# Feed-forward products of a hybrid decoder trunk, formed from seven block products instead of eight

## The reference

```
def _swiglu(x, w_gu, w_down):
    a, b = jnp.split(x @ w_gu, 2, axis=-1)          # w_gu 1024 x 5632
    return (jax.nn.silu(a) * b) @ w_down            # w_down 2816 x 1024

for i in range(DEPTH):                              # 2
    x = x + 0.5 * _swiglu(_rmsnorm(x, norm_g[i, 0]), ffn_gu[i, 0], ffn_down[i, 0])
    x = x + mixer(_rmsnorm(x, norm_g[i, 1]))        # retention, then gated delta
    x = x + 0.5 * _swiglu(_rmsnorm(x, norm_g[i, 2]), ffn_gu[i, 1], ffn_down[i, 1])
return _rmsnorm(x, final_g), new states
```

## Time and profile before

| | |
|---|---|
| median of 3 runs | 2621.64 us (2612.52 to 2621.98) |
| span of the profiled execution | 2619.2 us |
| TensorE busy, matmuls | 2572.6 us, 98% |
| VectorE busy | 1264.2 us, 48% |
| ScalarE busy | 821.0 us, 31% |
| GpSimd busy | 300.5 us, 11% |
| HBM traffic | 93 GB/s over the span |

### The profile page before, as it was taken

One profiled execution on the slowest core, in us unless ns is written; L12 is line 12 of the kernel. 1 busy time (PEld: TensorE's weight loads), 2 busy tenths in 40 slices (PEclk: granted clock), 3 DMA queues, 4 the chain that ended last, 5 costly groups with the idle time before them and its releaser, 6 DMA issues.

```text
span 2619.2 us, 48630 instructions
## 1 busy us (share of the span) xinstructions
PE 2572.6 (98%) x20575; PEld 2484.8 (95%) x20575; DVE 1264.2 (48%) x1584; ACT 821.0 (31%) x1042; POOL 300.5 (11%) x307
## 2 busy tenths in 40 slices
PE   8999999999999999999999999999999998999998
PEld 8999999898989899999999999989998998999998
DVE  5444334646464654443244443377557755444422
ACT  4222222424242432222232222244433344222222
POOL 1000010202020210000000000002530353000000
PEclk9999999999999999999999999999999999999999
DMA  4332334524242333332343323321122111323232
GB/s 131 96 96 76 88 93 141 185 86 177 93 173 97 137 91 87 96 86 78 97 111 91 96 82 89 104 84 52 49 66 87 36 49 53 97 84 93 78 91 74
DMA packets 340333, 246.73 MB, mean 94 GB/s; under 512 B 9428, under 2 KB 320908, under 8 KB 340208
## 3 DMA queue, kind: packets, MB, share of 16 engines
q1 hardware_dynamic: 325856, 197.32, 25.6%
q0 software_dynamic: 14352, 47.58, 5.0%
HBM read 218.81 MB, written 26.05 MB: 93 GB/s over the span
## 4 chain that ended last, share of the span: by engine, by line
PE 95%; DVE 3%; ACT 1%; issue 0%; DMA 0%; SPq 0%; ACTq 0%; DVEq 0%
PE ps L743 61%; PE ps L934 17%; PE ps L1118 5%; PE ps L828 1%; PE ps L851 1%; PE ps L837 1%; PE ps L1062 1%; PE ps L1128 1%; PE ps L783 1%; PE ps L1099 1%; DVE wl L1672 1%; PE ps L1075 1%; PE ps L993 0%; DVE xl L1678 0%; DVE cv L2012 0%
## 5 line engine op out<-in xcount | busy, mean ns | idle before, releaser
L743 PE MATMUL ps<-xh,wh 128*128 128x260 f32 x2816 | 569.0, 283 | 3.7 <-DVE gate L2258 1.5
L743 PE MATMUL ps<-xh,wl 128*128 128x260 f32 x2816 | 568.3, 284 | 0.0
L743 PE MATMUL ps<-xl,wh 128*128 128x260 f32 x2816 | 567.5, 283 | 0.0
L1672 DVE TENSOR_TENSOR wl<-raw,wh 128x2048 fp32r<-128x2048 f32 (+1 forms) x204 | 428.7, 2102 | 266.7 <-ACT wh L1333 266.5
L1333 ACT ACTIVATE wh<-raw 128x2048 fp32r<-128x2048 f32 (+1 forms) x204 | 354.5, 1738 | 343.2 <-PE ps L743 189.2
L743 PEld LDWEIGHTS ps<-xh,wh 128*128 128x128 f32 x2816 | 435.4, 189 | 5.8 <-issue 2.7
L743 PEld LDWEIGHTS ps<-xh,wl 128*128 128x128 f32 x2816 | 435.1, 189 | 0.0
L743 PEld LDWEIGHTS ps<-xl,wh 128*128 128x128 f32 x2816 | 433.8, 189 | 0.0
L743 PE MATMUL ps<-hh,wh 128*128 128x260 f32 x1408 | 284.4, 283 | 0.0
L743 PE MATMUL ps<-hh,wl 128*128 128x260 f32 x1408 | 283.1, 282 | 0.0
L743 PE MATMUL ps<-hl,wh 128*128 128x260 f32 x1408 | 282.8, 282 | 0.0
(11 more groups left out here) (372 smaller groups left out, 2857.8 us busy)
## 6 DMA issues: line engine op xcount, KB each, us to landing
raw<-in_ffn_gu_dram SPq DMA_DIRECT2D x176, 512.0 KB, 4.9
raw<-in_ffn_down_dram SPq DMA_DIRECT2D x64, 384.0 KB, 3.5
raw<-in_ret_w_in_dram SPq DMA_DIRECT2D x48, 512.0 KB, 4.4
raw<-in_ffn_down_dram SPq DMA_DIRECT2D x64, 320.0 KB, 3.9
s_ring<-in_state_ret_dram POOLq DMA_DIRECT2D x32, 512.0 KB, 6.2
out_dram<-s_ring POOLq DMA_DIRECT2D x32, 512.0 KB, 3.4
raw<-in_gdn_w_in_dram SPq DMA_DIRECT2D x32, 512.0 KB, 4.5
raw<-in_ret_w_out_dram SPq DMA_DIRECT2D x16, 512.0 KB, 3.8
```

Source lines behind the costliest of these rows:

```text
L743: m_ = nc.tensor.matmul(ps[:, 2 * q + h, 0:HALF], w_, v[:, kt0 + t, h * HALF:(h + 1) * HALF], start=b_, stop=e_)
L1672: nc.vector.tensor_tensor(wl[:, s, 0:cols], raw[:, s, 0:cols], wh[:, s, 0:cols].bitcast(F32), ALU.subtract).then_inc(w_low, 1)
```

## The change

All four feed-forwards are rewritten. In each, two K tiles, two output tiles and two token halves make a 2 x 2 by 2 x 2 block product, which is formed by Winograd's form of Strassen's scheme from seven products instead of eight. One feed-forward becomes 38 unrolled jobs (NJ): 22 gate jobs (gate and up tile of one index are the two output tiles; 4 pairs of K tiles) mixed with 16 down jobs (4 pairs of output tiles, in four rounds over the pairs of inner tiles that are ready: 2, 3, 3 and 3).

- TensorE: `products_of` gives the order of products in job j: 1, 2, 5, 6, then 4 of the job before, 3, 7. Each product is kp pairs x 3 passes of 128 x 128 x 260 into one bank; products 6, 3, 7 and 4 add onto what stands there.
- GpSimd: `block_sum` forms four sums of weight blocks per job, in order 1, 3 (for the job after the next), 2, 4 (for the next). It also forms sums T1 to T4 of the four blocks of h of a pair, `XG` for a down job, and the sums of squares.
- ScalarE and VectorE: `block_split` forms high and low parts of seven weight blocks per job in groups A (two blocks), 1, 2, 4, L (two); `h_split` those of the seven blocks of h of a pair, in three groups; `x_split` those of x ahead of a feed-forward.
- ScalarE copies the running sums out of a bank (m1, m5, u2); VectorE forms the outputs from banks and copies (C11, C12, C22, hA, hB; X11, X12, X21, X22 for down). The lower right output's last sum (C22) is formed by VectorE from the bank of product 7 and the copy m5.
- The mixers keep their code; their buffers move to other places.

```diff
+def ffn_jobs():
+    out = []
+    for q0, q1, pairs_ in ((0, 6, (0, 1)), (6, 12, (2, 3, 4)), (12, 18, (5, 6, 7)), (18, 22, (8, 9, 10))):
+        out += [("G", q, (0, 1, 2, 3)) for q in range(q0, q1)] + [("D", m, pairs_) for m in range(4)]
+    return out
+def products_of(j):
...
+    return [(j, 1), (j, 2), (j, 5), (j, 6), (j - 1, 4), (j, 3), (j, 7)]
...
+            def block_sum(f, j, n):                                    # GpSimd
+                r_, s_ = raw_blocks(f, j), mixed_block(j)
+                a11, a12, a21, a22 = r_[:, 0, :, 0, :], r_[:, 0, :, 1, :], r_[:, 1, :, 0, :], r_[:, 1, :, 1, :]
+                tt = nc.gpsimd.tensor_tensor
...
+                    m_ = tt(s_, a21, a22, ALU.add)
+                if n == "3":
+                    m_ = tt(a21, a11, a21, ALU.subtract)
+                if n == "2":
+                    pool.wait_ge(blk_low, blocks_split(f, j, "A"))
+                    pool.wait_ge(blk_sum, blocks_summed(f, j, "1"))
+                    m_ = tt(a11, s_, a11, ALU.subtract)
+                if n == "4":
+                    pool.wait_ge(blk_low, blocks_split(f, j, "1"))
+                    pool.wait_ge(blk_sum, blocks_summed(f, j, "2"))
+                    m_ = tt(s_, a12, a11, ALU.subtract)
...
+                for j in range(NJ + 1):                                # GpSimd, ffn
...
+                    if odd:
+                        v(f"hB.{b}")
...
+                        did(tt(parts[:, 6, :], parts[:, 5, :], parts[:, 2, :], ALU.subtract), f"T3.{e}")
+                        own(f"T1.{e}")
+                        did(tt(parts[:, 7, :], parts[:, 5, :], parts[:, 1, :], ALU.subtract), f"T2.{e}")
...
+                    if nxt:
+                        block_sum(*nxt, "2")
+                    if odd and j != LATE:
+                        fourth()
+                    if gated_b and not odd:
...
+                        did(tt(parts[:, 1, :], parts[:, 2, :], parts[:, 0, :], ALU.subtract), f"T1.{e}")
+                    if nxt:
+                        block_sum(*nxt, "4")
+                    if j > LATE:
+                        square_added(NORM_OUT[f], 2 * (j - LATE - 1))
+                    if j < NJ and not is_gate(j):
...
+                        did(tt(xt, xt, kept[:, 0:2, :], ALU.add), f"XG.{j}")
+                    if nxt2:
+                        block_sum(*nxt2, "1")
+                        block_sum(*nxt2, "3")
...
+                def product(c, m, steps=None):                         # TensorE
...
+                    o = ps[:, bank_of(c, m), 0:HALF]
+                    for t in steps:
...
+                        for n, (w_, r_) in enumerate(((hi_w, high), (hi_w, low), (lo_w, high))):
+                            m_ = nc.tensor.matmul(o, w_, r_, start=m in (1, 2, 5) and t == 0 and n == 0,
+                                                  stop=t == kp - 1 and n == 2, skip_group_check=m in (3, 4, 6, 7))
...
+            def block_split(f, j, group):                              # VectorE
+                dve.wait_ge(blk_high, blocks_split(f, j, group))
+                nc.vector.tensor_tensor(split_ends(wl, j, group), split_from(f, j, group), split_ends(wh, j, group).bitcast(F32),
+                                        ALU.subtract).then_inc(blk_low, 1)
...
+                for j in range(NJ + 1):                                # VectorE, ffn
...
+                    if j:
+                        t_(f"7.{b}")
+                        act_(f"m5.{b}")
+                        if gated_b:
+                            did(tt(kept[:, 2, :], bank(b, 7), kept[:, 3, :], ALU.add), f"C22.{b}")
...
+                    if gated_b:
+                        scaled_by_norm(b, "sr")
+                    if j:
...
+                        lower_second(b)
...
+                    if j < NJ:
+                        upper(j)
+                    low("A")
+                    low("1")
+                    if ending:
+                        tile_done(f, 2 * m)
+                    low("2")
+                    if odd:
+                        h_split(2, e)
+                    if j:
+                        lower(b)
+                    if j < NJ:
+                        upper_second(j)
...
+                    low("4")
...
+                    if is_gate(j):
+                        scaled_by_norm(j, "gr")
+                    if ending:
+                        tile_done(f, 2 * m + 1)
+                    if gated_b:
+                        h_split(3 if odd else 1, e)
+                    low("L")
...
```

More of the change, by code:

```diff
@@ new lines, in ffn_a_names @@
+def ffn_a_names():
+    out = []
+    for j in range(NJ):
+        b, gated = j - 1, is_gate(j - 1)
+        e, odd = (JOBS[b][1] // 2, JOBS[b][1] % 2) if gated else (0, 0)
+        out += ([f"silu.{b}"] if gated else []) + [f"m1.{j}", f"m5.{j}"]
+        if j == LATE:
+            out += [f"k2.{e}", f"k3.{e}", f"u2.{j}"]
+            continue
+        out.append(f"u2.{j}")
+        if odd:
+            out.append(f"k2.{e}")
+        if gated:
+            out.append(f"k3.{e}" if odd else f"k1.{e}")
+    return " ".join(out)
@@ new lines, in ffn_p_names @@
+def ffn_p_names():
+    out = []
+    for j in range(NJ + 1):
+        b, gated = j - 1, is_gate(j - 1)
+        e, odd = (JOBS[b][1] // 2, JOBS[b][1] % 2) if gated else (0, 0)
+        if gated:
+            out += [f"T3.{e}", f"T2.{e}", f"T4.{e}"] if odd else [f"T1.{e}"]
+        if j < NJ and not is_gate(j):
+            out.append(f"XG.{j}")
+    return " ".join(out)
+FFN_T = Steps(" ".join(f"{m}.{c}" for j in range(NJ) for c, m in products_of(j)))
+FFN_V = Steps(ffn_v_names())
+FFN_A = Steps(ffn_a_names())
@@ new lines, in build, with x_parts, raw_blocks @@
+            mixed = sb("mixed", [P, 2, BLOCK], stack=st)
+            parts = sb("parts", [P, 8, HALF], stack=st)
+        with ExitStack() as st:
+            sb("pair_below", [P, 15520], stack=st)
+            more_parts = [sb(f"parts{n}", [P, 8, HALF], stack=st) for n in range(2)]
+        NORM_IN, NORM_OUT = (0, 2, 3, 5), (1, 3, 4, 6)
+        def x_parts(f, m):
+            return parts if f == 2 else (parts, *more_parts)[m % 3]
+        def raw_blocks(f, j):
+            kind, _, pairs_ = JOBS[j]
+            if kind == "G":
+                return raw[:, j % 2, :].rearrange("p (m t two c) -> p m t two c", m=2, two=2, c=P)
+            return raw[:, j % 2, 0:4 * P * len(pairs_)].rearrange("p (t two m c) -> p m t two c", m=2, two=2, c=P)
@@ L525, in _ @@
+            ffn(0)
+            ret_body(phases[0], 0)
+            with sp.Fori(1, RH) as h:
+                ret_body(phases[0], h)
+            ffn(1)
+            ffn(2)
+            for g in range(2):
+                gdn_body(phases[1], g)
+            ffn(3)
             for c, (done, n) in enumerate(((y_by_v, 1), (y_by_a, 1), (y_by_v, 2), (y_by_v, 3))):
@@ L1413, in ret_body @@
                         split_next(5 + g // 2)
-                for n in range(KT):
-                    if n == 3:
-                        split_next(7)
-                    if last:
-                        act.wait_ge(acc_free, ph.unit0 + RET_UNITS * h + 12 + n + 1)
-                        scaled(ph.norm, n, n % 2, False)
+                if not last:
+                    split_next(7)
+                else:
+                    for n in range(KT):
+                        before_ffn(1, n)
             def gdn_pre_after(n):
@@ L1659, in _ @@
+            ffn(0)
+            ret_body(phases[0], 0, False)
+            with act.Fori(1, RH - 1) as h:
+                ret_body(phases[0], h, False)
+            ret_body(phases[0], RH - 1, True)
+            ffn(1)
+            ffn(2)
+            root_of(phases[1].norm - 1)
+            for g in range(2):
+                gdn_body(phases[1], g, g == 1)
+            ffn(3)
+            y_copied(KT - 1)
             act.wait_ge(ssq_sum, 7)
@@ L1858, in ret_body @@
                         split_next(6)
-                    if n == 3:
+                    if n == 3 and not last:
                         split_next(7)
                     if last:
-                        scaled_low(ph.norm, n)
+                        before_ffn(1, n)
             def pre_did(m_, name):
@@ L1946, in split_next @@
                 def split_next(j):
[L1947 to L1948 removed]
+                    split(ph.slot0 + GDN_SLOTS * g + j + 1, (j + 1) % 2)
                 def t_(name):
@@ L2285, in _ @@
+            ffn(0)
+            ret_body(phases[0], 0, False)
+            with dve.Fori(1, RH - 1) as h:
+                ret_body(phases[0], h, False)
+            ret_body(phases[0], RH - 1, True)
+            ffn(1)
+            ffn(2)
+            gdn_pre(phases[1])
+            for g in range(2):
+                gdn_body(phases[1], g, g == 1)
+            ffn(3)
             dve.wait_ge(y_roots, 2)
```

997 lines of the change are left out of this document (648 added, 349 removed).

## The result

The changed kernel takes 3073.37 us (median of four runs, 3072.98 to 3073.56), beside 2617.08 us for the kernel before on the same chip: a ratio of 1.1758, interval 1.1725 to 1.1791. The direction was forecast, the size was not: 2903 us was forecast, and 3073 lies above the range of 2680 to 3030.

The account below looks back on a forecast made before the run. The port pair that GpSimd and two-SBUF-input VectorE operations lock was taken to pace the kernel: 2619.2 + 236.8 for four feed-forwards (+59.2 each) + 45 for edges = 2901, plus 2.4 to the runs' median: 2903 us, range 2680 to 3030.

Parts of the forecast that it names:

- Bound and direction: Feed-forwards: 396 fewer matmuls each, but paced by the port VectorE and GpSimd share, not TensorE; slower, chance 0.87.
- The lock: GpSimd operations and VectorE ones with two SBUF inputs run in succession: 1.15 us per 512 plus 1.04 ns a column.
- I take 13.5: Gate job's period, 13.5 us: near all in a row with half the PSUM sums covered (13.2), moved toward the hand layout.
- Down jobs and passages: Down jobs were taken at 8.8 us (three pairs) and 6.8 us (two pairs); the hand layout gave 9.0 and 6.9.
- The last jobs: End of each feed-forward: two square sums and two scaled tiles add 3.4 us to each of three jobs, 10.2 us.
- The edges: Before and after the feed-forwards: +7 at the start, +6 and +13 at two, 19 for ends and joint; +45 (30 to 60).
- edges above 60 us: Sign against the forecast: it is wrong if the added time at the feed-forwards' edges exceeds 60 us.
- Rival 3: Feed-forward jobs take the full hand layout: gate 14.3, down 9.0 and 6.9 us, edges +50; 2990 us, chance 0.22.
- Rival 1: Every gate job: meetings don't bind, TensorE does; 2456 us, chance 0.1 together with what lies between.
- Rival 2: Feed-forwards take port time alone, orders mesh, starts and PSUM sums vanish under GpSimd; 2667 us, chance 0.2 with up to 2800.
- Rival 4: Matmuls don't fall by an eighth, or their pace worsens past 160 ns; above 3000 us, chance 0.03.
- the bounds of 0.58 and 1.27: GpSimd's sum of 260 columns, without a row: 0.58 us by columns to 1.27 us; +1.4 on a gate job at worst.

Follow-up runs that it names:

- e4: The changed kernel without the third of three passes of every feed-forward product (3696 of 11088 matmuls): 3053.03 us, 1.1668 of the kernel before.
- e1: The changed kernel with GpSimd's four weight sums per job cut to 4 columns of every block of 128: 2660.25 us, 1.0196 of the kernel before.
- e2: The changed kernel with low parts of weights in three feed-forwards subtracting a PSUM bank instead of the high part: 2915.78 us, 1.1176 of the kernel before.
- e3: The changed kernel, all work kept, with sum 4 right behind sum 2 and hA, C12 and gate scaling ahead of low part 2: 2916.26 us, 1.1178.
- e10: The changed kernel with each GpSimd sum of squares cut to 4 of its 520 columns: 3035.47 us, 1.1601 of the kernel before.
- e7: The order of e3 with the weight sums cut to 4 columns as in e1: 2574.75 us, 0.984 of the kernel before.
- e6: e3 with the four weight sums of each job on VectorE in place of GpSimd, all work done: 2785.78 us, 1.0678 of the kernel before.

## Why the forecast was too low

Both spans are of one execution, 2619.2 and 3071.8 us. Cut at the first and last C22 of each feed-forward (37 intervals of 38 jobs; before, the 3072 matmuls of the earlier trace rows), the miss of 3071.8 - 2901 = 170.8 us lies here:

| stretch | reckoned | measured |
|---|---|---|
| four steady stretches, 37 jobs each | 4 x 426.5 = 1706 | 454.5 + 474.0 + 458.2 + 459.3 = 1846.0 |
| to the first C22, over before | +7 and 2 for the first job | +29.9 |
| after retention | +6 and 2 | +19.1 |
| after the delta net | +13 and 2 | +20.5 |
| all else (ends, joint, mixers) | +19 and 2 | +14.1 |

The 2 us are a first job at 13.5 for 11.54. "Reckoned" is the prediction's own sum, cut at the same places.

**Bound and direction: right.** 1584 matmuls fewer, TensorE no bound (e4), VectorE and GpSimd the pace (e1). ScalarE and DMA were rightly given no price of their own, though ScalarE's copies of 0.63 are links between the two.

**The lock: right, in kind and price.** In the job above, sums 2 and 3 end 1.15 us after the low part that they met, and the scaling of 520 columns 0.56 after the sum (1.04 ns a column make 0.54); e2 takes the lock away from the low parts and finds the times alone.

**"I take 13.5": the step that failed.** Three figures stood there: 13.2 for all in a row with half the PSUM sums covered, 13.3 and 15.3 (mean 14.3) laid out by hand in program order, and 13.5 between, near the first. Measured: 13.76 and 15.37, mean 14.57. The layout was right to 0.5 and 0.1 us. e3 comes nearest to what the first figure describes: with the queues reordered a job takes 12.85. So the order of the queues, with its two waits per job, costs 14.57 - 12.85 = 1.7 us and was entered at 13.5 - 13.2 = 0.3. The value was moved only part of the way from 13.2 toward the layout, and no row stood behind that fraction, while the waits were traced through the code operation by operation. On the 14 full gate intervals of a feed-forward, 1.07 us x 14 x 4 is 60 of the 140 us by which the steady stretches were missed. The other seven gate intervals hold work of down jobs too; if each of these gate jobs is dearer by the same 1.07, the step is worth 90 (an estimate).

**Down jobs and passages: too low.** The other 19 intervals before the last four, seven reckoned as gate jobs and twelve as down jobs, were reckoned at 7 x 13.5 + 8 x 8.8 + 4 x 6.8 = 192.1 us in each feed-forward; over the four they sum to 807.4 for 768.4, 39 of the 140. Part of it is the same 13.5. The nine intervals between down jobs alone measure 8.89 for 8.1 (six at 8.8, three at 6.8).

**The last jobs: a term mis-sized.** The last four intervals of a feed-forward are down jobs and were reckoned at 4 x 8.8 + 10.2 = 45.4 us; over the four they sum to 222.8 for 181.6, 41 of the 140. The first feed-forward has 49.2; the second, with the next one's x parts in the same queues, 67.4. The prediction had this joint among its edges, and "all else" in the table is 6.9 us under in turn. The first of the last four (LATE), in which the last gate job is finished too, alone takes 18.5 and 20.5 us in them. Why it takes so much wasn't tried.

**The edges: a term mis-sized.** 53 us by this account, 83.6 measured; most of the difference is at the start, 29.9 for 9. The prediction named edges above 60 us as a sign that it was wrong; they came to 75.6 without the 2 us of each first job. The mixes were reckoned at 0.34 each, their pitch alone. They meet the squares and the first weight sums, and e10 shows the squares' part: 8.0 us at the start, some 30 us at all edges. The chain shows a second term, which the prediction didn't price. In order of time, after retention, at the joint of the second and third feed-forward, and after the delta net:

```profile
1077.10 3.42 DVE rinv L2271
...
1574.76 3.42 DVE rinv L2271
...
2591.11 3.40 DVE rinv L2271
```

This is VectorE's reciprocal for the norm. It is not new, but the chain of the kernel before has it at the first feed-forward alone (30.23, 3.42 us), and at these three places not. What it costs there was not tried. What of the rest is VectorE's own new work and what meetings with weight sums is open.

**Rivals.** Rival 3, the full layout (2990 us, chance 0.22), named the mechanism: order and lock together. It too falls short, by 83 us: 0.27 us on the 56 full gate intervals is 15 of it, the last jobs (38) and the edges (23) most of the rest. Rival 1 is nearest in e7, where TensorE is busy nearly throughout the gate jobs; even there the time is 2575, not 2456. Rival 2, port time alone, needs orders that mesh: e3 tries one, and stays above it at 2916. Rival 4 fell: the matmuls did fall by an eighth, and they run at their pace (below).

## What to carry to other kernels

- A scheme that trades matmuls for element-wise sums must be priced on the engines that do the sums, with their shared lock, before the matmuls saved are counted: here matmuls of 190 us were traded for weight sums that e1 puts at 413 us, waits included.
- Idle GpSimd is no free capacity beside a VectorE of two-input SBUF work. Four sums a job ran 130 us faster on VectorE, though it was the fuller engine (e6 for e3).
- Where queues are strictly in order and a producer-consumer chain crosses three engines, lay one period out by hand and believe it: here the layout was within 0.5 us. An overlap without a row behind it is no reason to shade a layout down. Where two causes bind at nearly the same point, removing either alone shows less than its share (1.34 and 1.72 us alone, 4.13 together).

## What the runs showed of the hardware

TensorE's clock fell around a short idle time, and it didn't matter. In the kernel after (start, us, instruction):

```profile
83.20 0.28 PE L1545 MATMUL ps<-xch,wl 128*128 128x260 f32 x1
86.67 0.47 PE L1545 MATMUL ps<-xch,wh 128*128 128x260 f32 x1 [3.19 <-DVE parts L2207]
86.94 0.42 PE L1545 MATMUL ps<-xcl,wh 128*128 128x260 f32 x1
...
90.47 0.28 PE L1545 MATMUL ps<-xch,wh 128*128 128x260 f32 x1
90.58 0.28 PE L1545 MATMUL ps<-xcl,wh 128*128 128x260 f32 x1
```

Before the 3.19 us without work matmuls follow each other at 0.12 us, after it at 0.217, the 1.2 GHz level (granted clock 0.53 over 86.6 to 90.1), and from 90.3 on at 0.12 again. e4 has 0.79 over its window and its periods are no longer for it.

Twelve passes into one bank, with one weight load each, keep the pace: e7's window has 1751 matmuls in 215 us, 122.8 ns each with all waits.

GpSimd's sum of 260 columns takes 0.74 us alone (L770 above, mean of 44: 0.745) between the bounds of 0.58 and 1.27 that the prediction set.
